# Fused attention in float32 on one core: where the softmax weights are normalised

## What is computed

```python
def diff_attend(qb, k, v, lam):                  # layer 0, 4 head pairs
    s = einsum('bqhcd,bkhd c...', qb, k) * ATTN_SCALE
    p = softmax(s, -1)
    a = p[:, :, 0] - lam * p[:, :, 1]
    return einsum('bhqk,bkhe->bqhe', a, v)

def gqa_attend(qb, k, v):                        # layer 0, 8 query heads
    p = softmax(einsum(qb, k) * ATTN_SCALE, -1)
    return einsum(p, v)
```

## Time and profile before

| what | value |
|---|---|
| runs | 3316.11 us median, 3311.89 to 3318.25 |
| span of the profiled execution | 3313.1 us |
| what lies around that span | not given for this execution; the median is 3.0 us above the span |
| mean granted TensorE clock | 0.944 |
| attention units of layer 0 | about 290.6 to 479.6 us of the span |
| attention units of layer 1 | about 1319.7 to 1478.9 us of the span |

### The profile page before, as it was taken

The page is one execution under the profiler, slowest core; times in us unless marked ns, Lnnn a source line. Parts: engine busy times, 40 slices in busy tenths (PEclk is TensorE's granted clock), DMA queues, the critical chain, the costliest instruction groups (busy, mean ns, idle before and its releaser), DMA issues. The chain is left out here.

```text
span 3313.1 us, 53803 instructions
## 1 busy us (share of the span) xinstructions
PE 2797.7 (84%) x22107; PEld 1780.7 (54%) x22107; DVE 1347.6 (41%) x2648; ACT 780.2 (24%) x1519; POOL 548.0 (17%) x668
## 2 busy tenths in 40 slices
PE   7998889488866699887676765699999999999999
PEld 4555655344433345654333332345888777588853
DVE  3424856421111343656211111734664454355551
ACT  2224651021111321540111111421212331211100
POOL 0002640233322100540322222010000100100000
PEclk9999999699988899998888988799999999999999
DMA  8733012899999751114999997422222112422337
GB/s 312 309 151 119 1 77 89 348 398 426 426 426 426 297 127 58 43 57 162 376 423 425 424 423 319 174 77 85 77 86 82 62 51 76 115 77 77 127 127 266
DMA packets 188539, 679.29 MB, mean 205 GB/s; under 512 B 52766, under 2 KB 94222, under 8 KB 163782
## 3 DMA queue, kind: packets, MB, share of 16 engines
q1 hardware_dynamic: 176446, 655.56, 50.7%
q0 software_dynamic: 11808, 21.03, 1.7%
q10 hardware_dynamic: 104, 0.10, 0.0%
HBM read 653.89 MB, written 33.98 MB: 208 GB/s over the span
## 5 line engine op out<-in xcount | busy, mean ns | idle before, releaser
L1756 DVE TENSOR_TENSOR hh<-hs,pH 128x128 f32<-128x128 f32 x118 | 33.9, 287 | 776.7 <-ACT hs L1739 776.7
L1719 PE MATMUL pH<-w,room 128*32 128x256 f32 x4224 | 258.7, 400 | 53.0 <-DMA w<-in_moe_w 51.9
L1719 PE MATMUL pH<-room 128*32 128x256 f32 x3328 | 214.6, 416 | 91.5 <-DMA room<-in_moe_w 68.6
L942 POOL TENSOR_SCALAR E<-E,st 128x768 f32<-128x768 f32 (+3 forms) x80 | 168.0, 2100 | 645.7 <-DVE st L1192 645.1
L1719 PEld LDWEIGHTS pH<-w,room 128*32 128x32 f32 x4224 | 142.8, 115 | 159.2 <-issue 79.3
L1719 PEld LDWEIGHTS pH<-room 128*32 128x32 f32 x3328 | 115.3, 120 | 183.3 <-issue 100.3
L419 PE MATMUL pa<-aT,w 128*128 128x512 f32 x416 | 205.6, 599 | 1.3 <-DVE aT L693 1.3
L1727 PE MATMUL pY<-w,hT 128*32 128x256 f32 x2112 | 128.3, 384 | 73.9 <-DVE hT L1759 64.3
L987 PE MATMUL pT<-ident,E 128*128 128x128 f32 x672 | 114.6, 290 | 54.8 <-ACT PT L1097 31.3
L1727 PE MATMUL pY<-room,hT 128*32 128x256 f32 x1664 | 100.6, 382 | 54.3 <-DVE hT L1759 54.3
L2105 PE MATMUL pa<-hT,ring 128*128 128x512 f32 x320 | 143.8, 606 | 0.0
(11 more groups left out here) (611 smaller groups left out, 5155.0 us busy)
## 6 DMA issues: line engine op xcount, KB each, us to landing
w<-in_moe_w SPq DMA_DIRECT2D x144, 2048.0 KB
room<-in_moe_w SPq DMA_DIRECT2D x48, 2048.0 KB
mw<-in_mod_w SPq DMA_DIRECT2D x24, 2048.0 KB, 16.7
ring<-in_w_ff_down SPq DMA_DIRECT2D x33, 1024.0 KB, 4.8
ring<-in_w_in SPq DMA_DIRECT2D x15, 2048.0 KB, 8.3
ring<-in_w_gate SPq DMA_DIRECT2D x6, 2048.0 KB, 8.1
wf<-in_w_ff_gate SPq DMA_DIRECT2D x11, 1024.0 KB, 5.7
wf<-in_w_ff_up SPq DMA_DIRECT2D x11, 1024.0 KB, 8.1
```

What stands on the lines that cost most here:

```text
L942: pool.tensor_scalar(e, e, st[:, u % 4, 6 + b:7 + b], None, ALU.mult).then_inc(readyP, 1)
L1719: last = pe.matmul(pH[strip(s), 0:2 * P].rearrange("p (j n) -> p j n", j=2), xT[:, k, :], slot_of(g, "w13", b)[:, :, k, s * P:(s + 1) * P] ...
L1756: dve.tensor_tensor(hh[:], hs[:], pH[:, P:2 * P], ALU.mult).then_inc(gated, 1)
```

## The change

The exponentials in `E` are no longer touched after ScalarE wrote them. GpSimd writes for each unit two 128x128 diagonal matrices into `fT` (which stands unused until the routing part): the identity times the reciprocal sum of head 0 and of head 1, the second times minus lambda for a differential unit. TensorE turns a block by a matmul with the block as the stationary operand and the diagonal as the moving one. For a differential unit it runs two such matmuls per key block, adding the second into the same PSUM place. VectorE keeps the reciprocals alone: the multiplication of head 0, the product with lambda and the subtraction are gone, and so are the semaphores `divided`, `readyD` and `readyP`. VectorE always runs `shift(u + 3)` before `invert(u + 2)` now.

```diff
+        def diagonal(u, b):
+            return fT[:, u % 4 * 2 + b, :]
@@ gpsimd
+            def weights(u):
+                (n, p), s = where(u), st[:, u % 4]
+                pool.wait_ge(inverted, u + 1)
+                if u >= 4:
+                    pool.wait_ge(turned, round_no(u - 3, 0))
+                pool.tensor_scalar(diagonal(u, 0), ident[:], s[:, 6:7], None, ALU.mult)
+                if p < diff:
+                    pool.tensor_scalar(diagonal(u, 1), ident[:], s[:, 7:8], lam[:, 5:6], ALU.mult, ALU.mult).then_inc(weights_ready, 1)
+                else:
+                    pool.tensor_scalar(diagonal(u, 1), ident[:], s[:, 7:8], None, ALU.mult).then_inc(weights_ready, 1)
@@ in the loop over u
-                b = 0 if where(u)[1] < diff else 1
-                e = E[:, u % NB, b, 0:width(u)]
-                pool.wait_ge(divided, u + 1)
-                pool.tensor_scalar(e, e, st[:, u % 4, 6 + b:7 + b], None, ALU.mult).then_inc(readyP, 1)
+                weights(u)
@@ tensor, turn
-                    pe.wait_ge(readyD, u + 1)
-                    pe.wait_ge(readyP, u + 1)
+                    pe.wait_ge(weights_ready, u + 1)
...
-                    last = pe.transpose(pT[:, tile(j)], E[:, u % NB, b, tile(i)], ident[:])
+                    if where(u)[1] < diff:
+                        pe.matmul(pT[:, tile(j)], E[:, u % NB, 0, tile(i)], diagonal(u, 0), start=True, stop=False)
+                        last = pe.matmul(pT[:, tile(j)], E[:, u % NB, 1, tile(i)], diagonal(u, 1), start=False, stop=True)
+                    else:
+                        last = pe.matmul(pT[:, tile(j)], E[:, u % NB, b, tile(i)], diagonal(u, b), start=True, stop=True)
@@ vector
-            def divide(u):
+            def invert(u):
...
                 dve.wait_ge(e_ready, u + 1)
-                dve.reciprocal(s[:, 6:8], s[:, 4:6]).then_inc(divided, 1)
-                dve.wait_ge(divided, u + 1)
-                if p < diff:
-                    step(dve.tensor_tensor(s[:, 8:9], s[:, 7:8], lam[:, 5:6], ALU.mult))
-                else:
-                    e = E[:, u % NB, 0, 0:width(u)]
-                    dve.tensor_scalar(e, e, s[:, 6:7], None, ALU.mult).then_inc(readyD, 1)
-
-            def subtract(u):
-                n, p = where(u)
-                if u < U and p < diff:
-                    e = E[:, u % NB, 0, 0:width(u)]
-                    dve.wait_ge(readyP, u + 1)
-                    dve.scalar_tensor_tensor(out=e, in0=E[:, u % NB, 1, 0:width(u)], scalar=st[:, u % 4, 8:9], in1=e,
-                                             op0=ALU.mult, op1=ALU.add).then_inc(readyD, 1)
+                if u >= 4:
+                    dve.wait_ge(weights_ready, u - 3)
+                dve.reciprocal(s[:, 6:8], s[:, 4:6]).then_inc(inverted, 1)
@@ vector, before and in the loop over u
-            divide(0)
+            invert(0)
             shift(2)
-            divide(1)
-            subtract(0)
+            invert(1)
...
-                subtract(u + 1)
                 move(u, 0)
-                if u + 2 < U and where(u + 2)[1] < diff:
-                    divide(u + 2)
-                    shift(u + 3)
-                else:
-                    shift(u + 3)
-                    divide(u + 2)
+                shift(u + 3)
+                invert(u + 2)
```

More of the change, by code:

```diff
@@ L858, in attention_phase @@
             ph.sem(n) for n in ("first_in", "const_in", "const_set", "lam_sum", "lam_exp", "rows_made"))
-        shared, scored0, scored1, shifted, e_ready, divided, readyD, readyP = (
-            ph.sem(n) for n in ("shared", "scored0", "scored1", "shifted", "e_ready", "divided", "readyD", "readyP"))
+        shared, scored0, scored1, shifted, e_ready, inverted, weights_ready = (
+            ph.sem(n) for n in ("shared", "scored0", "scored1", "shifted", "e_ready", "inverted", "weights_ready"))
         turned, moved, weighed, o_out = (ph.sem(n) for n in ("turned", "moved", "weighed", "o_out"))
```

## The result

The changed kernel takes 3394.73 us (median of 4 runs, 3390.72 to 3397.98) against 3316.26 before: slower, ratio 1.0243, 95% interval 1.0228 to 1.0257. The median moved by 78.5 us where 78.4 were forecast. The two profiled executions differ by a little more: the spans are 3395.8 and 3313.1 us, 82.7 apart, and the one after is the longest of its four runs.

The account below looks back on a forecast made before the run. TensorE's records, and its chain with ScalarE's copies, were taken to bound attention: 98.6 us of added records less 20.2 us of waits gave +78.4 us on 3316.1, so 3394.5 us, range 3370 to 3408.

Parts of the forecast that it names:

- context units: Layer 0's context tiles: 80 added records cost 8.8 us, less 5.3 us of waits that go.
- start of layer 0: First turn 4.0 us earlier, added records up to 2.0 dearer at the halved clock; taken as -3.3 us, ends 0 and -5.
- start of layer 1: First turn 1.4 us earlier, clock uncertain for the first two units: between +1.2 and -6, taken as -2 us.
- What bounds it: Attention: TensorE's own work in differential units, a TensorE-ScalarE chain in grouped-query units; idle time there hides no added records.
- The count of records: Block turns on TensorE in both layers: 560 + 336 = 896 records more.
- their price: Each added TensorE record costs 0.11 us, as with the products with V: +98.6 us in all.
- The waits: Attention turns and copies held up by VectorE, GpSimd and ScalarE, and the starts: 20.2 us go, bounds 12 to 28.
- rival 3: At both starts the clock stays up, saving another 4 us in layer 1 and 2 in layer 0: 3389 us; chance 0.12.
- two bounds: Whole forecast: record price 0.105 to 0.115 us, 4.5 either way; waits 12 to 28 us, 8 either way.
- Rivals 1 and 2: 1: idle TensorE time takes grouped-query records, 3370 us, chance 0.08; 2: diagonal matmul costs one record's time, 3308 us, 0.02.
- Rival 4: GpSimd's diagonals cost 0.92 us or more and come late, notably in context units: 3400 to 3430 us; chance 0.08.
- rival 5: Transposes on TensorE really cost less than 0.11 us, rows showing only start-up: 3432 us at worst; chance 0.02.

Follow-up runs that it names:

- the matmuls alone: The kernel before with each transpose replaced by a matmul with the identity, all scaling as before: 3389.32 us, ratio 1.0220.
- the kernel without scaling: The changed kernel with one transpose per block, no scaling or diagonals, second map left out: attention stretches 182.0 and 165.6 us.
- doubled transposes: The kernel before with every transpose issued twice into the same place: attention stretches grew by 27.1 and 32.3 us.
- late division: The kernel before with GpSimd out of differential units, VectorE subtracting unscaled exponentials, ScalarE's copy out of pO applying head 0's reciprocal: 3313.14 us, ratio 0.9990.

## Why the prediction was right, point by point

The terms, measured between unit starts in TensorE's timeline of the two kernels:

| part | predicted | measured |
|---|---|---|
| 15 latent differential units, records less waits | +29.7 - 7.8 = +21.9 | 86.9 - 63.4 = +23.5 |
| 16 latent grouped-query units | +21.1 - 1.3 = +19.8 | +22.4 |
| context units | +8.8 - 5.3 = +3.5 | +3.7 |
| start of layer 0, to the second unit's turn | +2.0 - 3.3 = -1.3 | -3.1 |
| start of layer 1, to the third unit's turn | +2.6 - 2.0 = +0.6 | -2.0 |
| rest of layer 1 | +34.3 - 0.5 = +33.8 | +38.6 |
| all else | 0 | -0.4 |
| sum | +78.3 | +82.7 |

**What bounds it** was right. The added records lie ahead of a copy which takes the whole round, so the idle 0.78 us stayed: shown by the bracket on both sides and by the matmuls alone.

**The count of records** was exact, **their price** too low. This term of the sum is the one that was mis-sized: 98.6 us, where the comparison with the kernel without scaling gives 107.8. I priced a matmul's record like a transpose's, at 0.11 us. The doubled transposes cost exactly that, 0.44 us a round of four blocks; matmuls in their place cost 0.50, mostly because such a round starts more slowly. Part by part, against the kernel without scaling, the records cost 31.4 us for 29.7 in the latent differential units, 23.7 for 21.1 in the latent grouped-query units, 9.6 for 8.8 in the context units, 39.3 for 34.3 in the rest of layer 1, and 3.9 for 4.6 at the two starts.

**The waits** were too low as well: 24.7 for 20.2. By the same comparison they were right in the latent tiles, 7.8 and 1.3 us: the changed kernel has no turn there that waits for VectorE or GpSimd longer than 0.15 us, and the late vector copies are gone (the last three grouped-query units of each of the first three tiles take 7.04 us each, those included that took 6.2 before). What they were was only half seen: of the 3.1 us in each of the third and fourth quads some 2 go with the subtractions that stood beside a row operation, as the second quad, which has none, lost 1.1. Subtractions and waits go all the same, so the sum isn't touched by it. The context units gave 5.9 for 5.3, the rest of layer 1 0.6 for 0.5. The main difference lies in the starts, 9.1 for 5.3, where I took values nearer the middle. Part of rival 3 came true: the clock came back sooner. Mean granted clock, from the windows view of the first stretch (columns as in the earlier trace rows), before:

```profile
280.00:300.00 20.00, 11.34 (x55) 7.63 (x54) 12.86 (x27) 10.67 (x23) 7.60 (x4) 0.74 0.93 299
```

and after:

```profile
280.00:300.00 20.00, 15.23 (x96) 12.31 (x93) 10.67 (x21) 10.50 (x22) 3.11 (x6) 0.91 0.91 293
```

With the records priced 9.2 us too low, the waits 4.5 us too low and -0.4 elsewhere the sum was 4.3 off the traces, and the runs happened to lie another 4 us closer. The prediction's two bounds, 4.5 and 8 us, add up to 3382 to 3407 and not to 3384 to 3406; the range holds either.

**The rivals.** Rivals 1 and 2 fell. Rival 4 didn't decide: a diagonal takes 0.61 us, and in the context tiles units (the first and the last apart) repeat after 2.0 to 2.3 us, near the 2.2 of TensorE's work. Its sign, a bracket with POOL, stands on the turns of the last two of them, with 0.38 and 0.47 us. For rival 5 the doubled transposes settle the price: 0.11 us each. That transposing is 4 times faster for float32, as the Trainium skill has it in "TensorE: Matmul & The Clock Gate", section "Terms", is not what this chip shows: a 128x128 block takes 0.11 us transposed and 0.22 us as a matmul, twice.

## What to carry to other kernels

Moving an elementwise operation into matmuls is free only if TensorE has time at that place in its chain. Look at what TensorE idles for: if it is the copy of the very round that gets longer, the idle time takes nothing, however large it is. When an engine is waited for, compare the operation that it was at with the same operation elsewhere: here one was three times as long beside unrelated work on GpSimd. And a transpose that turns into a float32 matmul doubled in price here, so before paying that, look for the place where a scale costs little, such as the copy out of PSUM of an output with its rows on the partitions (0.37 us with the scale here, 0.28 without).

## What the runs showed that was not expected

**The clock at layer 0's start follows the idle time, not the kind of instruction.** In the kernel before with matmuls for transposes, TensorE waits before layer 0's first turn as long as before, and the mean clock from 280 to 300 us is the same 0.74:

```profile
280.00:300.00 20.00, 11.34 (x53) 8.00 (x51) 12.32 (x24) 8.20 (x17) 6.62 (x3) 0.74 0.89 290
```

In the kernel with transposes alone, whose first turn comes early, it is 0.91 as in the changed one:

```profile
280.00:300.00 20.00, 15.40 (x90) 11.37 (x88) 12.48 (x24) 14.53 (x32) 0.00 (x0) 0.91 0.92 293
```

The Trainium skill, "TensorE: Matmul & The Clock Gate", section "PE-mode transpose", says that transposes don't count towards the full clock. In layer 0 these two runs show no difference by the kind; in both stretches scores run among the transposes, so a stretch of transposes alone is not tested. In layer 1 neither explains it. The first turn waits 4.85 us in the kernel before, with matmuls in place of transposes, and with doubled transposes; the mean clock over the same 20 us (1313 to 1333 in the earlier trace rows) is 0.66, 0.83 and 0.91, and the first two units take 15.1, 15.8 and 14.0 us. The late division, whose layer 1 is the same code as before, shows 4.85 us and 0.66 again. With so few profiles the cause stays open.

**A second scalar makes GpSimd's operation shorter.** The diagonal from one product took 0.61 us, the one with two 0.44, in every unit looked at (means 616 and 448 ns over layer 0). It isn't the place in the pair: a grouped-query unit's second diagonal, with one scalar, takes 0.60 us. I have no explanation.

**A smaller saving of time in the runs than in the stretches.** The late division saved 4.7 us of the two stretches and 2.7 of the runs; the difference is within what the runs of one kernel scatter (3305.46 to 3315.88).
